# First block's attention of a two-block transformer kernel, taken two maps at a time

## The reference

```python
qa, ka, va, qb, kb, vb, qc, kc, vc, fz = jnp.split(proj, cuts, axis=-1)
# A: 4 heads, each with two maps of width 32; o = (p1 - lam * p2) v, then a norm per head
a = p[:, :, 0] - lam * p[:, :, 1]
oa = oa * lax.rsqrt(jnp.mean(oa * oa, axis=-1, keepdims=True) + SUBLN_EPS)
# B: 6 heads, a mixture of three banded patterns (distances 1, 4 and 16)
# C: 6 heads with a forget gate
logf = jax.nn.log_sigmoid((fz + forget_bias).astype(jnp.float32))
cum_logf = lax.cumsum(logf, axis=1).transpose(0, 2, 1)
s = s + fq[..., :, None] - cum_logf[..., None, :]
s = jnp.where(kpos[None, :] <= qpos[:, None], s, -jnp.inf)
o = jnp.concatenate([merge(oa), merge(ob), merge(oc)], axis=-1)
return o @ w_out
```

## Time and profile before

| | us |
|---|---|
| median of three runs | 2077.4 (2076.44 to 2081.32) |
| the profiled execution's own time | 2079.4 |
| its span in the trace | 2077.5 |
| mean granted clock of TensorE | 0.901 |
| busy: TensorE, VectorE, ScalarE, GpSimd | 1682.1, 539.4, 305.8, 89.6 |

### The profile page before, as it was taken

How to read it: one execution, slowest core, us unless ns; L and a number is a source line. 1 busy time by engine, 2 the same in 40 slices (tenths; PEclk the granted TensorE clock), 3 DMA queues, 4 the chain that set the end, 5 groups by cost and what they waited for, 6 DMA issues and landing times.

```text
span 2077.5 us, 19648 instructions
## 1 busy us (share of the span) xinstructions
PE 1682.1 (81%) x8220; PEld 907.3 (44%) x8220; DVE 539.4 (26%) x1204; ACT 305.8 (15%) x797; POOL 89.6 (4%) x116
## 2 busy tenths in 40 slices
PE   7999999999999999999856665555899856665665
PEld 3576888544668884457412121111456311121211
DVE  1674466312354220235301010000164200010101
ACT  1243100011430000126200000000134200000000
POOL 0011000000110000031000000000120000000000
PEclk9999999999999999999988787887999887787868
DMA  9890897645306640464599999999943899999997
GB/s 360 291 314 2 262 326 276 228 138 202 121 11 204 202 162 21 164 196 200 238 422 421 421 422 422 422 422 422 326 159 152 353 421 421 422 422 422 421 422 311
DMA packets 184328, 599.63 MB, mean 289 GB/s; under 512 B 18753, under 2 KB 77761, under 8 KB 135105
## 3 DMA queue, kind: packets, MB, share of 16 engines
q1 hardware_dynamic: 184014, 598.10, 74.4%
q10 hardware_dynamic: 242, 0.53, 0.1%
HBM read 594.81 MB, written 3.80 MB: 288 GB/s over the span
## 4 chain that ended last, share of the span: by engine, by line
PE 58%; DMA 36%; DVE 3%; ACT 2%; issue 1%; POOL 0%; DVEq 0%; SPq 0%; ACTq 0%; POOLq 0%
PE ps L923 14%; DMA extra<-in_w_down 13%; DMA extra<-in_w_up 12%; DMA extra<-in_w_gate 10%; PE ps L767 8%; PE ps L952 8%; PE ps L1231 7%; PE ps L993 6%; PE ps L1131 3%; PE ps L903 3%; PE ps L660 2%; PE ps L682 2%; PE ps L670 1%; DVE extra L1837 1%; PE ps L723 0%
## 5 line engine op out<-in xcount | busy, mean ns | idle before, releaser
L1231 PE MATMUL ps<-ring,wide 128*32 128x512 f32 x2240 | 349.9, 781 | 218.3 <-DMA ring<-in_w_down 94.2
L923 PE MATMUL ps<-hT,ring 128*128 128x256 f32 (+1 forms) x1664 | 311.1, 349 | 0.0
L923 PEld LDWEIGHTS ps<-hT,ring 128*128 128x128 f32 x1664 | 278.1, 192 | 34.9 <-issue 4.9
L1231 PEld LDWEIGHTS ps<-ring,wide 128*32 128x32 f32 x2240 | 82.8, 138 | 467.2 <-issue 223.5
L1231 PE MATMUL ps<-extra,wide 128*32 128x512 f32 x784 | 137.7, 837 | 94.0 <-DMA extra<-in_w_down 37.7
L767 PE MATMUL ps<-ring,hT 128*128 128x512 f32 (+1 forms) x448 | 176.4, 550 | 2.0 <-ACT hT L1311 2.0
L952 PE MATMUL ps<-ring,wide 128*128 128x512 f32 x352 | 157.3, 608 | 7.9 <-DVE wide L2088 7.9
L2404 DVE TENSOR_TENSOR wide<-ps,wide 128x512 f32<-128x512 f32 x16 | 10.3, 686 | 512.7 <-PE ps L1231 512.7
L993 PE MATMUL ps<-ring,hT 128*128 128x512 f32 (+2 forms) x320 | 127.3, 555 | 0.3 <-issue 0.3
L767 PEld LDWEIGHTS ps<-ring,hT 128*128 128x128 f32 x448 | 80.6, 193 | 92.6 <-issue 90.5
L1231 PEld LDWEIGHTS ps<-extra,wide 128*32 128x32 f32 x784 | 31.7, 147 | 199.0 <-issue 84.3
(11 more groups left out here) (263 smaller groups left out, 1409.3 us busy)
## 6 DMA issues: line engine op xcount, KB each, us to landing
ring<-in_w_gate SPq DMA_DIRECT2D x24, 4096.0 KB, 34.3
ring<-in_w_down SPq DMA_DIRECT2D x24, 4096.0 KB, 33.4
ring<-in_w_up SPq DMA_DIRECT2D x22, 4096.0 KB, 33.5
ring<-in_w_mod SPq DMA_DIRECT2D x24, 2048.0 KB, 13.0
ring<-in_w_up SPq DMA_DIRECT2D x44, 1024.0 KB, 8.1
extra<-in_w_gate SPq DMA_DIRECT2D x8, 4096.0 KB, 34.3
extra<-in_w_up SPq DMA_DIRECT2D x8, 4096.0 KB, 33.5
extra<-in_w_down SPq DMA_DIRECT2D x8, 4096.0 KB, 33.9
```

The costliest lines, as they stand in the source:

```text
L923: last = mm(ps[2 * (j % 2) + half][:, f * T + o:f * T + o + n], wt[:, k, w:w + P], h8[:, k, o:o + n], start=k == 0, stop=k == KD - 1)
L1231: last = mm(ps[bank + n][e * CAP:(e + 1) * CAP, :], lhs[:, k, e * CAP:(e + 1) * CAP], expert_at(n0, e, k % PAIR, n * N), start=k == 0, sto ...
```

## The change

The maps are taken in ten pairs: 0 to 2 are of B, 3 to 6 of A (the two maps of one head), 7 to 9 of C. Step p of the loop issues the scores of pair p + 2, the flips of pair p and the values of pair p - 1.

- Keys and queries are stored flipped in one buffer `qkT`, with one ScalarE copy of 512 columns for each flip. A map's score uses only the rows of its own head: 64 partitions for B and C, 32 for A. The two maps of a pair have different rows and write into different banks. Their instructions stand in turn.
- The mask, in units of the unscaled score, is added and the row maxima are taken in one VectorE instruction (`tensor_tensor_reduce`, L2013), one for each block of query rows. The exponential applies the scale.
- The forget sums are computed once with six columns of weights, at partitions 0 and 32. ScalarE copies them into `crow`. A product of six rows with a column of the identity adds them to each C score. GpSimd's biases go.
- VectorE copies the flipped probabilities of the second map of each pair, ScalarE those of the first.
- The flips of four pairs' head outputs stand within the flips of pairs 2, 3, 4 and 9; the first group of the output projection is cut into pieces, between which the last flips stand.
- The first pair's scores stand between the two halves of the last input projection, and its maxima and exponentials follow there.
- Modulations 8 and 9 of layer 0 use banks 2 and 3.

```diff
+HEADS_AT = {2: 0, 3: 1, 4: 2, 9: 7}
+PAIRS1 = [("B", i) for i in range(BH // 2)] + [("A", i) for i in range(AH)] + [("C", i) for i in range(CH // 2)]
+QK_BLOCK = {"A": (0, 2), "B": (4, 7), "C": (10, 13)}
...
+        qkT = qk[:, 0:4096].rearrange("p (b t) -> p b t", b=16)
...
+        def half1(p, e):
+            kind, i = PAIRS1[p]
+            qb_, kb_ = QK_BLOCK[kind]
             if kind == "A":
+                return dict(q=qb_ + i // 2, k=kb_ + i // 2, at=64 * (i % 2) + 32 * e, n=32, scale=32 ** -0.5, v=B1_V["A"] + HD * i)
+            return dict(q=qb_ + i, k=kb_ + i, at=64 * e, n=64, scale=HD ** -0.5, v=B1_V[kind] + HD * (2 * i + e))
...
+                def score1(p):
+                    if p >= 2:
+                        pe.wait_ge(*s.at("att_max_ready", 2 * p - 2))
+                    for c, (o, n) in enumerate(CAUSAL_KEYS):
+                        if PAIRS1[p][0] == "C":
+                            for e in range(2):
+                                hd = 2 * PAIRS1[p][1] + e
+                                pick = ident[32 * e:32 * e + CH, 32 * e + hd:32 * e + hd + 1].to_broadcast([CH, P])
+                                mm(ps[(4, 0)[p % 2] + e][:, o:o + n], pick, crow[32 * e:32 * e + CH, 0:n], start=True, stop=False)
+                        for e in range(2):
+                            h = half1(p, e)
+                            v = slice(h["at"], h["at"] + h["n"])
+                            last = mm(ps[(4, 0)[p % 2] + e][:, o:o + n], qkT[v, h["q"], c * P:(c + 1) * P], qkT[v, h["k"], 0:n],
+                                      start=PAIRS1[p][0] != "C", stop=True)
+                    last.then_inc(s.up("att_scores_done"), 1)
+                def head_flip1(p, c, to):
+                    return nc.tensor.transpose(to, proj1[:, c, head_cols(p):head_cols(p) + P], ident)
+                def flip1(p):
+                    for e in range(2):
+                        m = 2 * p + e
+                        pe.wait_ge(*s.at("att_probs_ready", m + 1))
+                        if p >= 1:
+                            pe.wait_ge(*copied1(s, p - 1, e))
+                        if p - 1 in HEADS_AT:
+                            pe.wait_ge(*s.at(("b1_heads_by_act", "b1_heads_by_dve")[e], sum(q < p for q in HEADS_AT)))
+                        for i in range(3):
+                            last = nc.tensor.transpose(ps[6 + e][:, i * P:(i + 1) * P], pr1[:, m % 4, i * P:(i + 1) * P], ident)
+                        if p in HEADS_AT:
+                            pe.wait_ge(*s.at("att_out_read", HEADS_AT[p] + 1))
+                            last = head_flip1(HEADS_AT[p], e, ps[6 + e][:, 3 * P:4 * P])
+                        last.then_inc(s.up("att_probs_flipped"), 1)
+                def weigh1(p):
+                    out_ = ps[2 + p % 2]
+                    if p >= 2:
+                        pe.wait_ge(*s.at("att_out_read", p - 1))
+                    for e in range(2):
+                        pe.wait_ge(*copied1(s, p, e))
+                    for e in range(2):
+                        v = half1(p, e)["v"]
+                        for i, (c, kc) in enumerate(blocks):
+                            o = (2 * e + c) * HD
+                            last = mm(out_[:, o:o + HD], pT1[:, (2 * p + e) % 4, i * P:(i + 1) * P], proj1[:, kc, v:v + HD],
+                                      start=kc == 0, stop=kc == c)
+                    last.then_inc(s.up("att_values_done"), 1)
+                def cumsum():
+                    pe.wait_ge(*s.at("b1_forget_ready", 1))
+                    n2 = nlf.rearrange("p (c h) -> p c h", c=2)
+                    for o in (0, 32):
+                        mm(ps[3][o:o + CH, 0:T], n2[:, 0, :], tri[:, 0:T], start=True, stop=False)
+                        last = mm(ps[3][o:o + CH, P:T], n2[:, 1, :], tri[:, 0:P], start=False, stop=True)
+                    last.then_inc(s.up("b1_cumsum_done"), 1)
...
+                        if i == 6:
+                            pe.wait_ge(*s.at("b1_mod_ready", 8))
+                            pe.wait_ge(*s.at("b1_qk_ready", 5))
+                            score1(0)
                         linear1(i, j, 1, ks)
...
+                for p in range(NP1):
+                    if p + 2 < NP1:
+                        if p + 2 == FIRST_C:
+                            pe.wait_ge(*s.at("b1_cumsum_ready", 2))
+                        score1(p + 2)
+                    flip1(p)
+                    if p >= 1:
+                        weigh1(p - 1)
+                pe.wait_ge(*s.at("att_max_ready", 2 * NP1))
+                pe.wait_ge(*s.at("b1_heads_by_act", 3))
+                pe.wait_ge(*s.at("b1_heads_by_dve", 3))
+                out1(0, 0, (2, 3, 4))
+                pe.wait_ge(*s.at("b1_diff_ready", 1))
+                for k in range(2):
+                    for c in range(2):
+                        last = nc.tensor.transpose(ps[4 + k][:, c * P:(c + 1) * P], proj1[:, c, k * P:(k + 1) * P], ident)
+                last.then_inc(s.up("b1_heads_flipped"), 1)
+                weigh1(NP1 - 1)
+                pe.wait_ge(*s.at("b1_heads_by_act", 4))
+                pe.wait_ge(*s.at("b1_heads_by_dve", 4))
+                out1(0, 0, (5,))
...
-                            for e in range(n):
-                                av(kT[:, kb0 + n * (o - w) + e, :], src, ACT.Copy, scale=tb(rows_of)[:, e:e + 1])\
+                    av(qkT[:, 2 * u:2 * u + 2, :], ps[6 + u % 2][:, :].rearrange("p (b t) -> p b t", b=2), ACT.Copy)\
+                        .then_inc(s.up("b1_qk_ready"), 1)
...
+                act.wait_ge(*s.at("b1_cumsum_done", 1))
+                for o in (0, 32):
+                    av(crow[o:o + CH, :], ps[3][o:o + CH, 0:T], ACT.Copy, scale=HD ** 0.5).then_inc(s.up("b1_cumsum_ready"), 1)
+                for p in range(1, NP1 + 1):
+                    if p < NP1:
+                        exps1(p)
+                    copy1(p - 1)
...
+                def mask1(p):
+                    for e in range(2):
+                        m = 2 * p + e
+                        dve.wait_ge(*s.at("att_scores_done", p + 1))
+                        if p >= 2:
+                            dve.wait_ge(*s.at("att_probs_flipped", m - 3))
+                        src, dst = ps[(4, 0)[p % 2] + e], pr1[:, m % 4, :]
+                        bias = mult if PAIRS1[p][0] == "B" else causal
+                        for c, (o, n) in enumerate(CAUSAL_KEYS):
+                            nc.vector.tensor_tensor_reduce(dst[:, o:o + n], src[:, o:o + n], bias[:, o:o + n],
+                                                           -half1(p, e)["scale"], 3.0e38, ALU.add, ALU.min,
+                                                           nmx[:, 2 * m + c:2 * m + c + 1])\
+                                .then_inc(s.up("att_max_ready" if c else None), 1)
+                def copy1(p):
+                    m = 2 * p + 1
+                    dve.wait_ge(*s.at("att_probs_flipped", m + 1))
+                    if p >= 2:
+                        dve.wait_ge(*s.at("att_values_done", p - 1))
+                    cp(pT1[:, m % 4, :], ps[7][:, 0:3 * P]).then_inc(s.up("b1_probsT_by_dve"), 1)
+                    if p in HEADS_AT:
+                        cp(h8[:, head_block(HEADS_AT[p]), P:T], ps[7][:, 3 * P:4 * P]).then_inc(s.up("b1_heads_by_dve"), 1)
...
-                    stt(dst, src, mp["scale"], bias, ALU.mult, ALU.add).then_inc(s.up("att_scores_read"), 1)
-                    dve.wait_ge(*s.own())
-                    for c, (o, n) in enumerate(CAUSAL_KEYS):
-                        nc.vector.tensor_reduce(nmx[:, 2 * m + c:2 * m + c + 1], dst[:, o:o + n], AX.X, ALU.max,
-                                                negate=True).then_inc(s.up("att_max_ready" if c else None), 1)
...
+                for p in range(NP1 + 1):
+                    if p + 1 < NP1:
+                        mask1(p + 1)
+                    if p < NP1:
+                        copy1(p)
+                    if p == NP1:
+                        dve.wait_ge(*s.at("b1_heads_flipped", 1))
+                        cp(h8[:, 0, :], ps[4][:, 0:T]).then_inc(s.up("b1_heads_by_dve"), 1)
+                    if p >= 1:
+                        out1(p - 1)
```

More of the change, by code:

```diff
@@ L323, in two_blocks @@
         nbias = gbuf[:, :].rearrange("p (h c k) -> p h c k", h=NAH, c=2)
-        fbias = [qk[:, o + (P + T) * i:o + (P + T) * (i + 1)] for o, k in ((4096, 4), (512, 2)) for i in range(k)]
-        nfrow = hT[:, 0:1536].rearrange("p (h k) -> p h k", h=CH)
         cT = qk[:, 1536:2304].rearrange("p (b t) -> p b t", b=3)
@@ L635, in _ @@
             pe.sem_inc(tile_done, SLOTS)
-            def transpose_chunk(c, src, j):
-                for k in (2 * j, 2 * j + 1):
-                    o = (2 * (k % 2) + c) * P
-                    last = nc.tensor.transpose(ps[4 + j][:, o:o + P], src(k, c), ident)
-                return last
-            def transpose_8(s, src, name):
-                for j in range(4):
```

(33 more changed lines are left out.)

248 lines of the change are left out of this document (97 added, 151 removed), and 4 rows, old and new, of the table B1_COUNT.

## The result

The changed kernel takes 2069.98 us (median of five runs, 2069.54 to 2073.32) beside 2081.32 for the kernel before on the same chip (2076.44 to 2082.05): ratio 0.9956, 95% interval 0.9940 to 0.9971, 9 us faster. A second set of it gave 0.9951 [0.9937, 0.9965]. The forecast was 2064.5 from a kernel before at 2077.4; the measured time lies in the forecast's range of 2050 to 2077, and the direction was right. Of the expected gain of 12.9 us, about 4 are missing by the ratio (9.2 us), and fewer by the two medians (11.3); the absolute times lie further apart because the kernel before itself measured 3.9 us slower than the value that the forecast began from. The profiled execution has its own time 2073.32 and a span of 2071.5; the spans of the other four were 2067.7 to 2068.7.

The account below looks back on a forecast made before the run. TensorE was taken to bound the attention stretch, with VectorE close behind. A layer's steps summed to 49.2 us against 54.8 and 56.5, gaining 5.6 and 7.3, together 12.9: 2079.4 to 2066.5, less 2.0 to the median, 2064.5; range 2050 to 2077.

Parts of the forecast that it names:

- What bounds the kernel, and that nothing saved is lost: Whole chain: TensorE has 58% of the span, transfers 36%; the second block's expert transfers move whole with first-block savings.
- Scores side by side, loads one after another (0.84): A pair's eight score instructions on TensorE: streams overlap, weight loads do not, 8 x 0.105 = 0.84 us.
- Rival B: Pair scores on TensorE: loads overlap too, scores 0.65 us, no cost of changing tiles; 2053 us in all, chance 0.22.
- Rival C: Pair scores on TensorE: rows do not overlap, scores 1.42 us; 2080 us in all, no change, chance 0.13.
- Changing between tile heights in C: Steps 5 to 7, C's scores with forget sums: three more tile changes of 0.16 us, 4.3 us a step.
- The fused mask: VectorE mask and maxima in one pass: 0.7 us for half a pair, leaving VectorE covered by TensorE.
- rival D: VectorE's fused mask is dear: at 1.5 us a half a layer's gain is gone, at 2.0 it is 2092; chance 0.10.
- Forget sums: Layer's head on TensorE: eight instructions on six columns, taken as 1.1 us, 1.3 if alone.
- Steps 8 and 9, and the end: Last steps 7.7 us, TensorE idle for 3.7 of it behind VectorE and ScalarE; then output, flips and values 9.1 us.
- rival E: TensorE's clock falls after the 3.7 us idle time, 3.3 us lost in each layer: 2071 us in all, chance 0.10.
- A: The main case, the step-by-step sum: 49.2 us a layer, 2064.5 us in all, own range 2058 to 2071, chance 0.45.
- The chances: Whole kernel: faster, below 2071.2, 0.71; within 0.3% (6.2 us) 0.19; slower 0.10.

Follow-up runs that it names:

- best: Changed kernel with forget sums copied later, A's joining split and spread, three output products before the last flips, last values before A's head flips: 13.3 us under the changed kernel.
- no_pick: Changed kernel without the products that add the forget sums to C's scores: ratio moved by 0.0012 to 0.0017, some 3 us faster.
- full_rows: Changed kernel with each score product over all 128 rows, giving other scores than the reference: ratio 0.9988 to the kernel before, changed kernel 0.9951 on that chip.
- unfused: Changed kernel with mask and maxima as separate VectorE instructions and score scaling left out: ratio 0.9979 to the kernel before, changed kernel 0.9951 on that chip.
- fill_idle: Changed kernel with four unused 512-column products in TensorE's wait before pair 9's flips: ratio lower by 0.0013 and 0.0018 than the changed kernel's two sets.

## Why the prediction was right, and where its size was off

*What bounds the kernel, and that nothing saved is lost.* Right: 6.3 us at the start of the experts, 6.0 at the end, and 18.0 and 18.3 with best.

*Scores side by side, loads one after another (0.84).* The number came out, 0.85, and the mechanism behind it did not; that is luck. The loads overlap: the products of a pair's two maps start 7 ns apart, one of each map, as a couple. The four couples start at 557.719, 557.933, 558.044 and 558.263: the third follows the second, of 128 columns, after 0.11 us, and the fourth follows the third, of 256 columns, after 0.22. Two loads therefore pass in the time of one 128-column stream. The streams alone come to 0.65 us. The other 0.20 is the price of changing the tile size: the first couple's loads are not hidden behind the value products (0.214 us to the second couple instead of 0.11), and the first flip starts 0.304 us after the last couple instead of 0.22. With the 0.15 in the flips it is 0.35 a pair, where the prediction had 0.3 for changes and 0.84 for scores: 1.14 foreseen, 1.00 measured. The kernel before could have shown the overlap, as the weight loads of its column tiles also start 7 ns apart. The Trainium skill (TensorE: Matmul & The Clock Gate, "Packing small matmuls — row/col tiling") has the starts close together and the loads overlapping, and this trace agrees with both (7 ns, two loads in 0.105 us). Rival B was thus right on the loads and fell on its other half, no cost of changing: its 2.55 us a step and 0.35 make 2.9, and no_pick's step is 2.95. Rival C fell with the 0.85 itself; full_rows shows with 1.37 that its price of 1.42 without overlap was sound.

*Changing between tile heights in C.* The step was 4.19 against 4.3. The four groups take 0.42, 0.42, 0.63 and 0.63, 2.10 us together, where 0.84 + 0.84 for the products and 0.3 + 3 x 0.16 for the changes were reckoned, 2.46. Their streams come to 1.31, so each of the four groups pays 0.2 for its change, and no_pick, with one group for four, has 0.86. Again loads priced too high and changes too low nearly cancel.

*The fused mask.* 0.55, so rival D fell; unfused shows that VectorE does bound a middle step at 1.11.

*Forget sums.* 0.54 + 0.25 us, where 1.1 was taken. The head is 8.96 all the same, because ScalarE copies the sums (0.77) ahead of pair 1's exponentials and TensorE waits 0.85; the prediction had that order but no wait from it. The two errors cancel.

*Steps 8 and 9, and the end.* This is the term that was too small. The wait was right, in place and size: 3.92 us for 3.7, ended by ScalarE behind VectorE's joining and mask. The work behind it was priced at the upper clock: 7.7 + 9.1 = 16.8 us, measured 21.6. At that clock it takes 17.4 (fill_idle), so 4.2 us are the clock's and the sum without it, 49.5, meets the 49.2. That is rival E, which was held at 0.10 and priced at 3.3 us lost in each layer, 2071. It should not have been a rival to A but a term of it: nothing in E excludes A, and the earlier trace rows showed the clock falling behind smaller waits, at 0.78. Held so, the likeliest case would have been 2071, a gain of 6.3 us. That 2070 was measured is no proof of it, as the kernel before had by then measured 3.9 us slower. The gain of the stretches, 4.3 us, is what this account explains (12.3 without the clock's part, in fill_idle); the 9 us of the ratio lie between the two sums.

*The chances.* Faster by more than 0.3% at 0.71 came out, though the interval's upper end, 0.9971, just touches that bound.

What stays open: why one wait of 1.7 us is followed by a fall in one layer and not in the other; why the profiled pair differs by 6.0 us when the ratio says 9, and the stretches by 4.3; and why fill_idle, 8 us shorter in its two stretches, gains 3 to 4 by the ratios.

## What to carry to other kernels

When a change shortens the busy part of a stretch and leaves a wait of some microseconds in it, price the work behind that wait at both levels of TensorE's clock; here the wait cost 3.9 us itself and 4.2 more after it. Look for work that is ready and has a free bank, and put it into the wait: three output products, a reordered joining and a later copy of the forget sums gave more than the whole change had. Small products in separate rows run side by side with their loads, but each change of tile size costs time, here 0.35 us a pair where the streams side by side saved 0.65; so put the products of one tile size together. Make the engine beside them as fast as the new step, as the fused mask was. And when a measured row agrees with a sum, ask whether its parts agree too.

## What the runs showed of the hardware

- Score products over 32 or 64 rows, two side by side: 0.85 us for eight; the same one after another 1.50, over all 128 rows 1.37. The float32 loads of 128 columns pass two in 0.105 us when they are in different rows, and one in 0.11 when they are in the same.
- Changing the tile size between these scores and products over the whole array costs 0.35 us there and back (0.20 in the scores, 0.15 in the flips behind them), and 0.2 at each change between six-row and 64-row groups.
- With a pair's products one at a time in the same 32 or 64 rows, TensorE's clock fell to 1.2 GHz after at least 11 us without a gap and stayed there for 27 more without one (37.5 us in all); with 128-row products in the same places it stayed at 2.4 until the wait.
- With a wait of 3.9 us it stood at 1.2 GHz for 6.8 or 10.2 us, from within the wait or just behind it; after one of 2.2 us, seen once in a stretch at the upper level, for 3.4 us; after 1.7 for 6.8 us or not at all.
- Mask and minimum in one VectorE instruction from PSUM: 0.28 us for 128 columns, 0.42 for 256, with 0.08 for the read of the result; 0.55 for half a pair where mask and maxima apart took 1.11.
